# FFN input product of a two-layer encoder: seven half products for eight, over gate/up pairs

## Chip, cores and metric

One core of one Trainium2 chip runs the whole program in one launch. The metric is the device time of that launch in microseconds, lower is better.

## What is computed

A bidirectional encoder of `DEPTH` = 2 layers over T = 528 tokens (16 meta tokens and 512 of the input), model width 1024. Each layer has four token mixers, whose outputs are joined by one output projection, and then the feed-forward part, which is all that the change touches:

```python
def rms_norm(x, g):
    xf = x.astype(jnp.float32)
    y = xf * lax.rsqrt(jnp.mean(xf * xf, axis=-1, keepdims=True) + EPS)
    return (y * g.astype(jnp.float32)).astype(x.dtype)
...
        h = h + mixed @ w_out[l]
        hn = rms_norm(h, ffn_norm_g[l])
        gate, up = jnp.split(hn @ w_ffn_in[l], 2, axis=-1)
        h = h + (jax.nn.silu(gate) * up) @ w_ffn_out[l]
    return h[:, N_META:].astype(x.dtype)
```

`w_ffn_in` is 1024 x 5632: 22 tiles of 128 gate columns and 22 of 128 up columns (`KF` = 22). The last layer needs no meta tokens behind its output projection, so it works on 512 tokens there.

## The kernel before

All is held feature-major: a tile has 128 features on the partitions and the tokens along the free dimension. `h` holds the 8 tiles of the residual stream. Every fp32 product is made as three products of fp32r operands: each operand is split into a lead (the value cast to fp32r) and a rest (value minus lead), and lead x lead, lead x rest and rest x lead are summed in PSUM.

The weights come as a stream of slots of 128 x 1024 (512 KB), one for each output tile of 128 columns. SyncE loads slot by slot into `raw`, which has two places. For each slot ScalarE casts the lead into `parts` (`lead`, L1574), GpSimd subtracts it from the weights to get the rest (`rest`, L651), and TensorE multiplies. `parts` has two places too (`PARTS` = 2), so lead and rest of a slot are made while TensorE works on the slot ahead of it. A lead waits until TensorE has left the place (`w_used`), a load waits until GpSimd has made the rest (`split`).

The order of the work is written out by hand in one block for each engine, and each engine runs its instructions strictly in that order. TensorE's order behind the mixers, for each layer, is:

- eight groups of the second half of the output projection (`G_OUT2`). VectorE adds each to `h` (`residual`, L1944), multiplies by the norm's gain and splits the result into lead and rest (`gains`, L1895 and L1896). ScalarE squares `h` (L1454), VectorE adds the squares up (L1912);
- 44 groups of the FFN input product (`G_FIN`), gate and up in turn. A group is one output tile: 8 input tiles times 3 products. In the first layer the 528 tokens are two matmuls of 264 columns (`product`, L873, two banks of PSUM); in the last layer one of 512 (L908 to L910, one bank). Behind the first group comes the sum for the norm (`residual_sum`), from which ScalarE makes the scale `rstd` (L1474, L1475);
- eight groups of the output product (`G_FOUT`), 22 steps each.

For each gate/up pair j VectorE scales both groups out of PSUM (`scale_out`, L1927, into `ebuf` and `mbuf`), ScalarE applies Silu to the gate (L1862), VectorE multiplies the two (L2473) and splits the product into lead (L2475) and rest (L2476), the operand of the output product.

## Time and profile before

| | |
|---|---|
| median of 3 runs | 2173.76 us (2170.25 to 2173.88) |
| the profiled execution | 2173.68 us, of which 2171.8 us are the span of its instructions |
| TensorE busy | 2023.7 us, 93% of the span |
| GpSimd busy | 1001.7 us, 46% |
| VectorE busy | 1084.3 us, 50% |
| ScalarE busy | 831.0 us, 38% |
| mean granted TensorE clock | 0.986 |
| FFN input product, first layer | 725.9 to 985.9 us of the span |
| FFN input product, last layer | 1798.3 to 2044.1 us of the span |

In the profile an engine's busy time is the time covered by its instructions. PE is TensorE's matmuls, PEld its weight loads, DVE VectorE, ACT ScalarE, POOL GpSimd, SP SyncE. An instruction that has been issued and waits for a resource inside its engine counts as busy, so its row is longer than those of the same form. Times of rows are microseconds from the span's start. L12 is line 12 of the kernel. "pb" is PSUM; every other name is a buffer in SBUF.

### The profile page before, as it was taken

The numbers are of one execution on the slowest core, as the hardware profiler recorded it, in microseconds if no ns is written. First come the engines' busy times: TensorE is split into PE (matmuls) and PEld (weight loads), VectorE is DVE, ScalarE is ACT, GpSimd is POOL, SyncE is SP. The second block draws the span as 40 slices with busy tenths as digits, with TensorE's granted clock in tenths as the row PEclk, the third lists the DMA queues.
The fourth block names the chain that finished last, engine by engine and source line by source line (L and its number), as shares of the span: only waits on it lengthen the run. The fifth ranks groups of instructions, "written<-read, shape, count | busy, mean of one in ns | idle before, by whom it ended". The sixth has DMA issues, their size and how long they took to land.

```text
span 2171.8 us, 32558 instructions
## 1 busy us (share of the span) xinstructions
PE 2023.7 (93%) x13234; PEld 1755.5 (81%) x13234; DVE 1084.3 (50%) x1721; ACT 831.0 (38%) x1364; POOL 1001.7 (46%) x593
## 2 busy tenths in 40 slices
PE   7999998888789999999999999988887899999999
PEld 7988987567668999999999889885665677888887
DVE  7532377666665544441037332676656755444300
ACT  4322343677563222222234222444666622222211
POOL 4365444774323444444434455337853234444443
PEclk9999999999989999999999999999999999999999
DMA  4211111000001222223322111111001022233333
GB/s 168 69 59 59 59 49 69 10 1 30 20 20 59 89 88 93 92 88 97 98 81 85 59 59 59 52 57 40 1 20 30 20 78 97 89 96 97 97 101 113
DMA packets 40325, 143.80 MB, mean 66 GB/s; under 512 B 4592, under 2 KB 4976, under 8 KB 40048
## 3 DMA queue, kind: packets, MB, share of 16 engines
q1 hardware_dynamic: 40176, 141.72, 20.3%
q8 instruction: 106, 1.74, 0.3%
q14 instruction: 43, 0.35, 0.0%
HBM read 139.60 MB, written 2.10 MB: 65 GB/s over the span
## 4 chain that ended last, share of the span: by engine, by line
PE 75%; DVE 12%; ACT 7%; issue 5%; POOL 1%; DMA 0%; SPq 0%; DVEq 0%; ACTq 0%; POOLq 0%
PE pb L873 35%; PE pb L908 7%; PE pb L909 7%; PE pb L910 7%; PE pb L946 4%; PE pb L948 3%; PE pb L947 3%; DVE rowmax L2001 2%; PE pb L1331 1%; PE pb L1323 1%; ACT rstd L1480 1%; ACT ebuf L1515 1%; PE pb L1032 1%; ACT proj_r L1536 1%; POOL parts L651 1%
## 5 line engine op out<-in xcount | busy, mean ns | idle before, releaser
L651 POOL TENSOR_TENSOR parts<-raw,parts 128x1024 fp32r<-128x1024 f32 x248 | 606.8, 2447 | 797.0 <-ACT parts L1574 796.9
L1574 ACT ACTIVATE parts<-raw 128x1024 fp32r<-128x1024 f32 x248 | 262.5, 1058 | 832.3 <-PE pb L873 404.3
L873 PE MATMUL pb<-proj_r,parts 128*128 128x264 f32 x3104 | 427.9, 285 | 0.5 <-POOL parts L651 0.5
L873 PEld LDWEIGHTS pb<-proj_r,parts 128*128 128x128 f32 x3104 | 399.6, 189 | 0.8 <-issue 0.7
L873 PE MATMUL pb<-mix,parts 128*128 128x264 f32 x2208 | 332.5, 292 | 22.6 <-DVE mix L1903 13.6
L873 PEld LDWEIGHTS pb<-mix,parts 128*128 128x128 f32 x2208 | 298.1, 194 | 27.2 <-DVE mix L1903 14.0
L946 PE MATMUL pb<-mix,parts 128*128 128x264 f32 x800 | 242.6, 303 | 1.3 <-DVE proj L1936 1.3
L948 PE MATMUL pb<-mix,parts 128*128 128x264 f32 x800 | 229.5, 287 | 0.0
L947 PE MATMUL pb<-mix,parts 128*128 128x264 f32 x800 | 229.2, 286 | 0.0
L908 PE MATMUL pb<-proj_r,parts 128*128 128x512 f32 x528 | 207.4, 393 | 0.8 <-DVE mbuf L1927 0.8
L910 PE MATMUL pb<-proj_r,parts 128*128 128x512 f32 x528 | 207.7, 393 | 0.0
L909 PE MATMUL pb<-proj_r,parts 128*128 128x512 f32 x496 | 197.3, 398 | 0.0
L946 PEld LDWEIGHTS pb<-mix,parts 128*128 128x128 f32 x800 | 152.9, 191 | 14.2 <-issue 11.8
L1944 DVE TENSOR_TENSOR h<-h,pb 128x528 f32<-128x528 f32 (+1 forms) x48 | 33.1, 691 | 259.0 <-PE pb L910 134.2
L947 PEld LDWEIGHTS pb<-mix,parts 128*128 128x128 f32 x800 | 153.1, 191 | 0.9
L948 PEld LDWEIGHTS pb<-mix,parts 128*128 128x128 f32 x800 | 152.7, 191 | 0.0
L1927 DVE TENSOR_TENSOR mbuf<-pb,rstd 128x528 f32<-128x528 f32 (+1 forms) x44 | 30.8, 699 | 215.1 <-PE pb L873 110.8
L908 PEld LDWEIGHTS pb<-proj_r,parts 128*128 128x128 f32 x528 | 99.2, 188 | 24.9 <-DVE mbuf L1927 1.2
L910 PEld LDWEIGHTS pb<-proj_r,parts 128*128 128x128 f32 x528 | 99.3, 188 | 22.4
L2475 DVE CAST proj_r<-ebuf 128x528 fp32r<-128x528 f32 x44 | 110.8, 2518 | 1.5
L1936 DVE TENSOR_TENSOR proj<-pb,rstd 128x264 f32<-128x264 f32 x100 | 42.6, 427 | 137.9 <-PE pb L948 137.7
L909 PEld LDWEIGHTS pb<-proj_r,parts 128*128 128x128 f32 x496 | 94.0, 189 | 20.8
(290 smaller groups left out, 3291.9 us busy)
## 6 DMA issues: line engine op xcount, KB each, us to landing
raw<-w_stream SPq DMA_DIRECT2D x250, 512.0 KB, 3.5
w_head<-w_heads SPq DMA_DIRECT2D x8, 512.0 KB, 4.0
h<-x_t SPq DMA_DIRECT2D x8, 264.0 KB, 4.6
out_t<-h SPq DMA_DIRECT2D x8, 256.0 KB, 4.9
con<-consts SPq DMA_DIRECT2D x1, 1652.5 KB, 9.7
par<-params SPq DMA_DIRECT2D x1, 170.0 KB, 6.5
par<-params SPq DMA_DIRECT2D x1, 166.0 KB, 5.9
con<-consts SPq DMA_DIRECT2D x1, 128.0 KB, 6.4
```

Source lines behind the costliest of these rows:

```text
L651: nc.gpsimd.tensor_tensor(parts[:, n % PARTS, 1, :], w, parts[:, n % PARTS, 0, :].bitcast(FP32), ALU.subtract).then_inc(split.sem, 1)
L873: last = nc.tensor.matmul(pb[rows_, 2 * p + a, 0:HALF], lhs_t, rhs[:, a * HALF:(a + 1) * HALF], start=start, stop=stop)
L908: nc.tensor.matmul(o, w_lead, lead[:, kept(l, g)], start=(k == 0), stop=False)
L909: nc.tensor.matmul(o, w_lead, rest[:, kept(l, g)], start=False, stop=False)
L910: last = nc.tensor.matmul(o, w_rest, lead[:, kept(l, g)], start=False, stop=(k == k_all - 1))
L946: nc.tensor.matmul(o, w_lead, lead, start=(k == 0), stop=False)
L947: nc.tensor.matmul(o, w_lead, rest, start=False, stop=False)
L948: last = nc.tensor.matmul(o, w_rest, lead, start=False, stop=(k == KD - 1))
L1574: nc.scalar.activation(parts[:, n % PARTS, 0, :], raw[:, r % RAW, :], ACT.Copy).then_inc(lead_ready.sem, 1)
L1936: ins = nc.vector.tensor_tensor(dst[:, cut], pb[:, 2 * bank_pair(g) + a, 0:HALF], rstd[:, cut], ALU.mult)
L2001: link(nc.vector.tensor_reduce(rowmax[:, n % 2:n % 2 + 1], pair(n % 2), AX.XY, ALU.max))
L2475: link(nc.vector.tensor_copy(lead, prod))
```

## The change

The FFN input product is arranged as a 2 x 2 by 2 x 2 block product for each gate/up pair: the weight blocks are gate and up (rows) by the first and second half of the 1024 inputs (A11, A12; A21, A22), the operand blocks are the two halves of the inputs by the first and second half of the tokens. One level of Strassen's scheme (in Winograd's form) makes the four output blocks of 128 x 264 (128 x 256 in the last layer) from seven products in the place of eight. Each of the seven ("half product") is 4 input tiles times 3 matmuls of 264 or 256 columns into one PSUM bank. In the order in which they run their weights are A11, A12, A22, S1, S3, S2, S4 (i = 0 to 6; q = 7j + i), where

S1 = A21 + A22, S3 = A11 - A21, S2 = S1 - A11, S4 = A12 - S2.

- VectorE makes the four weight sums of a pair (`w_sums`, 128 x 512 each), mostly in place in the raw slots.
- Lead and rest are made for half slots (`lead_fin`, `rest_fin`): seven of 128 x 512 on ScalarE and seven on GpSimd for each pair, where there were two of 128 x 1024. `parts` becomes a ring of four half slots (`FIN_RING`).
- The up weights of all pairs use the same place in `raw`; the gate weights alternate between the other place and `sq`. SyncE loads the up weights of a pair when the rest of S3 of the pair before is made.
- The operand has 16 blocks in the place of 8 tiles: first, second, even and odd of each of four pairs of input tiles. ScalarE copies and casts (`x_copy`, `first_lead`, `second_lead`, `summed_lead`), VectorE makes the differences (`first_difference`, `other_differences`) and the rests (`b_rest`). The output projection's second half runs in the order `PAIRED`, so that both tiles of a pair are ready one after the other.
- Out of PSUM, ScalarE copies one product (`fin_copy`) and VectorE makes seven sums of 128 x 264, each of one PSUM bank and one SBUF operand (`fin_sums`), then multiplies gate and up by `rstd` in SBUF (`fin_scaled`). The product's lead is made by ScalarE (`product_lead`) and not by VectorE; the rest stays on VectorE (`product_rest`).
- In ScalarE's order the Silu of pair j - 1 (`gate_silu`) stands behind the lead of S3 and ahead of the lead of S2 of pair j. In VectorE's order the first three weight sums of pair j + 1 stand behind the first sum of pair j.
- Before the first slot of the output product GpSimd clears `kh` and `qh` in the first layer, since they held operand blocks.

The diff, cut to what the prediction speaks of:

```diff
+PAIRED = [f + KD // 2 * b for f in range(KD // 2) for b in range(2)]
+FIN_A11, FIN_A12, FIN_A22, FIN_S1, FIN_S3, FIN_S2, FIN_S4 = range(7)
+N_FIN = 7 * KF
+FIN_RING = 4
+B_FIRST, B_SECOND, B_EVEN, B_ODD = range(4)
...
+        def fin_split_of(layer, q):
+            r = (q + 2 * layer) % FIN_RING
+            return tuple(parts[:, r // 2, b, r % 2 * (SLOT // 2):(r % 2 + 1) * (SLOT // 2)] for b in range(2))
+        def fin_bank(layer, q):
+            return pb[:, (q + 6) % 8, 0:fin_half(layer)]
...
+                j = s - 1 - S_FIN
+                if j == 2:
+                    return added.sem, added.at(l, 2 * KD)
+                if j in (2 * KF, 2 * KF + 1):
+                    return fin_rest.sem, fin_rest.at(l, 7 * (KF - 1) + FIN_S3 + 1 if j % 2 else 7 * (KF - 2) + FIN_S4 + 1)
+                if 2 < j < 2 * KF:
+                    return fin_rest.sem, fin_rest.at(l, 7 * (j // 2 - 1) + FIN_S3 + 1 if j % 2 else 7 * (j // 2 - 2) + FIN_S4 + 1)
...
+                for q in range(N_FIN):
+                    rest_fin(l, q)
+                if l + 1 < DEPTH:
+                    pool.wait_ge(fin_used.sem, fin_used.at(l, N_FIN))
+                    nc.gpsimd.memset(kh[:, :, :], 0.0)
+                    nc.gpsimd.memset(qh[:, :, :], 0.0).then_inc(cleared.sem, 1)
+                for s in range(S_FOUT, N_SLOT):
+                    rest(l, s)
...
+            def fin_product(l, q):
+                j, i = q // 7, q % 7
+                pe.wait_ge(fin_rest.sem, fin_rest.at(l, q + 1))
+                if q in (0, 4, 6):
+                    pe.wait_ge(evac.sem, evac.at(l, G_FIN - {0: 2, 4: 1, 6: 0}[q]))
+                if q == 6:
+                    pe.wait_ge(rs_ready.sem, rs_ready.at(l, RS_F + 1))
+                if j and i == 1:
+                    pe.wait_ge(fin_copied.sem, fin_copied.at(l, j))
+                if j >= 2 and i == 0:
+                    pe.wait_ge(fin_read.sem, fin_read.at(l, 7 * (j - 1)))
+                if j and i in (2, 3, 4):
+                    pe.wait_ge(fin_read.sem, fin_read.at(l, 7 * (j - 1) + {2: 1, 3: 5, 4: 6}[i]))
+                w_lead, w_rest = fin_split_of(l, q)
+                o = fin_bank(l, q)
+                for c in range(KD // 2):
+                    if q < 4:
+                        pe.wait_ge(b_ready_f.sem, b_ready_f.at(l, 4 * c + q + 1))
+                    lead, rest = fin_operand(l, i, c)
+                    nc.tensor.matmul(o, w_lead[:, c * P:(c + 1) * P], lead, start=(c == 0), stop=False)
+                    nc.tensor.matmul(o, w_lead[:, c * P:(c + 1) * P], rest, start=False, stop=False)
+                    last = nc.tensor.matmul(o, w_rest[:, c * P:(c + 1) * P], lead, start=False, stop=(c == KD // 2 - 1))
+                last.then_inc(fin_used.sem, 1)
...
+                for q in range(N_FIN):
+                    fin_product(l, q)
+                    if q == 3:
+                        residual_sum(l, 2)
...
+            def lead_fin(l, q):
+                j, i = q // 7, q % 7
+                if i in (FIN_A11, FIN_A22):
+                    n = l * N_RAW + S_FIN + 1 + 2 * j + (i == FIN_A22)
+                    act.wait_ge(loaded[LOAD_AT[n][0]].sem, LOAD_AT[n][1])
+                if i >= FIN_S1:
+                    act.wait_ge(fin_summed.sem, fin_summed.at(l, 4 * j + i - FIN_S1 + 1))
+                if q < FIN_RING:
+                    act.wait_ge(w_used.sem, w_used.at(l, S_FIN - (1 if q < 2 else 0)))
+                else:
+                    act.wait_ge(fin_used.sem, fin_used.at(l, q - FIN_RING + 1))
+                nc.scalar.activation(fin_split_of(l, q)[0], fin_piece(l, q), ACT.Copy).then_inc(fin_lead.sem, 1)
...
+            def fin_copy(l, j):
+                act.wait_ge(fin_used.sem, fin_used.at(l, 7 * j + FIN_A11 + 1))
+                if j:
+                    act.wait_ge(fin_read.sem, fin_read.at(l, 7 * (j - 1) + 4))
+                nc.scalar.activation(fin_first[:, 0:fin_half(l)], fin_bank(l, 7 * j + FIN_A11), ACT.Copy).then_inc(fin_copied.sem, 1)
+            def gate_silu(l, j):
+                act.wait_ge(evac.sem, evac.at(l, G_FIN + 2 * j + 1))
+                g = ebuf[:, j % 2, 0:2 * fin_half(l)]
+                nc.scalar.activation(g, g, ACT.Silu).then_inc(gsilu.sem, 1)
+            def product_lead(l, j):
+                act.wait_ge(act_product.sem, act_product.at(l, j + 1))
+                nc.scalar.activation(act_parts(j)[0][:, fin_cut(l)], ebuf[:, j % 2, 0:2 * fin_half(l)], ACT.Copy).then_inc(act_lead.sem, 1)
...
                 for k in range(KD):
-                    lead(l, S_OUT2 + k + 2)
+                    if k < KD - 2:
+                        lead(l, S_OUT2 + k + 2)
+                    elif k == KD - 2:
+                        lead_fin(l, 0)
+                        lead_fin(l, 1)
+                    else:
+                        lead_fin(l, 2)
                     act.wait_ge(evac.sem, evac.at(l, G_OUT2 + k + 1))
+                    if k % 2 == 0:
+                        x_copy(l, k // 2)
+                        first_lead(l, k // 2)
+                    else:
+                        second_lead(l, k // 2)
+                        summed_lead(l, k // 2, B_EVEN)
+                        summed_lead(l, k // 2, B_ODD)
+                    if k == KD - 1:
+                        lead_fin(l, 3)
                     residual_square(l, 1, k)
-                residual_rstd(l, 1)
-                nc.scalar.preload_act_table_set("silu_and_others")
-                for j in range(KF):
-                    lead(l, S_FIN + 2 * j + 2)
-                    act.wait_ge(evac.sem, evac.at(l, G_FIN + 2 * j + 1))
-                    nc.scalar.activation(ebuf[:, j % 2, :], ebuf[:, j % 2, :], ACT.Silu).then_inc(gsilu.sem, 1)
-                    lead(l, S_FIN + 2 * j + 3)
+                for q in range(FIN_RING, N_FIN):
+                    j, i = q // 7, q % 7
+                    lead_fin(l, q)
+                    if i == 4:
+                        fin_copy(l, j)
+                        if j == 0:
+                            residual_rstd(l, 1)
+                            nc.scalar.preload_act_table_set("silu_and_others")
+                        else:
+                            gate_silu(l, j - 1)
+                    if i == 6 and j:
+                        product_lead(l, j - 1)
+                lead(l, S_FOUT)
+                lead(l, S_FOUT + 1)
+                gate_silu(l, KF - 1)
+                product_lead(l, KF - 1)
...
+            def w_sums(l, j, n):
+                gate, up, w = fin_gate(l, j), fin_up(l, j), SLOT // 2
+                a11, a12, a21, a22, s1 = gate[:, 0:w], gate[:, w:], up[:, 0:w], up[:, w:], fin_sum(j)
+                if n == 0:
+                    r = l * N_RAW + S_FIN + 1 + 2 * j
+                    dve.wait_ge(loaded[LOAD_AT[r + 1][0]].sem, LOAD_AT[r + 1][1])
+                    dve.wait_ge(loaded[LOAD_AT[r][0]].sem, LOAD_AT[r][1])
...
+                    if j > 1:
+                        dve.wait_ge(fin_rest.sem, fin_rest.at(l, 7 * (j - 1) + FIN_S1 + 1))
+                    ins = nc.vector.tensor_tensor(s1, a21, a22, ALU.add)
+                elif n == 1:
+                    ins = nc.vector.tensor_tensor(a21, a11, a21, ALU.subtract)
+                elif n == 2:
+                    dve.wait_ge(fin_rest.sem, fin_rest.at(l, 7 * j + FIN_A11 + 1))
+                    dve.wait_ge(fin_summed.sem, fin_summed.at(l, 4 * j + 2))
+                    ins = nc.vector.tensor_tensor(a11, s1, a11, ALU.subtract)
+                else:
+                    dve.wait_ge(fin_rest.sem, fin_rest.at(l, 7 * j + FIN_A12 + 1))
+                    dve.wait_ge(fin_summed.sem, fin_summed.at(l, 4 * j + 3))
+                    ins = nc.vector.tensor_tensor(a12, a12, a11, ALU.subtract)
+                ins.then_inc(fin_summed.sem, 1)
+            def fin_sums(l, j, n):
+                w = fin_half(l)
+                first, g, up = fin_first[:, 0:w], ebuf[:, j % 2, 0:2 * w], mbuf[:, j % 2, 0:2 * w]
+                i, own, dst, after = ((FIN_A12, first, g[:, 0:w], None), (FIN_S2, first, first, 1), (FIN_S3, first, up[:, w:2 * w], 2),
+                                      (FIN_S1, first, g[:, w:2 * w], 2), (FIN_A22, up[:, w:2 * w], up[:, 0:w], 3),
+                                      (FIN_S1, up[:, w:2 * w], up[:, w:2 * w], 5), (FIN_S4, g[:, w:2 * w], g[:, w:2 * w], 4))[n]
+                dve.wait_ge(fin_used.sem, fin_used.at(l, 7 * j + (i if n in (0, 6) else FIN_S2) + 1))
+                if n == 0:
+                    dve.wait_ge(fin_copied.sem, fin_copied.at(l, j + 1))
+                else:
+                    dve.wait_ge(fin_read.sem, fin_read.at(l, 7 * j + after))
+                nc.vector.tensor_tensor(dst, fin_bank(l, 7 * j + i), own, ALU.add).then_inc(fin_read.sem, 1)
+            def fin_scaled(l, j, buf):
+                at = buf[:, j % 2, 0:2 * fin_half(l)]
+                dve.wait_ge(fin_read.sem, fin_read.at(l, 7 * j + 7))
+                nc.vector.tensor_tensor(at, at, rstd[:, fin_cut(l)], ALU.mult).then_inc(evac.sem, 1)
...
+                    if k == KD - 1:
+                        for n in range(4):
+                            w_sums(l, 0, n)
+                    residual(l, G_OUT2 + k, PAIRED[k])
+                    if k % 2 == 0:
+                        first_difference(l, k // 2)
+                        b_rest(l, k // 2, B_FIRST)
+                    else:
+                        other_differences(l, k // 2)
+                        b_rest(l, k // 2, B_SECOND)
+                        b_rest(l, k // 2, B_EVEN)
+                        b_rest(l, k // 2, B_ODD)
                     add_square(l, 1, k)
                 dve.wait_ge(rs_ready.sem, rs_ready.at(l, RS_F + 1))
                 for j in range(KF):
-                    if j >= 2:
-                        dve.wait_ge(act_ready.sem, act_ready.at(l, j - 1))
-                    scale_out(l, G_FIN + 2 * j, ebuf[:, j % 2, :])
-                    scale_out(l, G_FIN + 2 * j + 1, mbuf[:, j % 2, 0:T])
+                    fin_sums(l, j, 0)
+                    if j + 1 < KF:
+                        for n in range(3):
+                            w_sums(l, j + 1, n)
+                    if j:
+                        product_rest(l, j - 1)
+                    for n in range(1, 6):
+                        fin_sums(l, j, n)
+                    if j + 1 < KF:
+                        w_sums(l, j + 1, 3)
+                    fin_sums(l, j, 6)
+                    fin_scaled(l, j, ebuf)
+                    fin_scaled(l, j, mbuf)
                     dve.wait_ge(gsilu.sem, gsilu.at(l, j + 1))
                     dve.wait_ge(evac.sem, evac.at(l, G_FIN + 2 * j + 2))
-                    prod = ebuf[:, j % 2, :]
-                    link(nc.vector.tensor_tensor(prod, prod, mbuf[:, j % 2, 0:T], ALU.mult))
-                    lead, rest = act_parts(j)
-                    link(nc.vector.tensor_copy(lead, prod))
-                    nc.vector.tensor_tensor(rest, prod, lead.bitcast(FP32), ALU.subtract).then_inc(act_ready.sem, 1)
+                    prod = ebuf[:, j % 2, 0:2 * fin_half(l)]
+                    nc.vector.tensor_tensor(prod, prod, mbuf[:, j % 2, 0:2 * fin_half(l)], ALU.mult).then_inc(act_product.sem, 1)
+                product_rest(l, KF - 1)
```

## Rows read from the trace of the kernel before

**Rows 1.** The page: busy time and instructions by engine.

```profile
PE 2023.7 (93%) x13234; PEld 1755.5 (81%) x13234; DVE 1084.3 (50%) x1721; ACT 831.0 (38%) x1364; POOL 1001.7 (46%) x593
```

**Rows 2.** Busy time by stretch: both input products, and attention.

```profile
core 0: us, PE busy (x) PEld busy (x) DVE busy (x) ACT busy (x) POOL busy (x), PEclk, DMA share, GB/s
725.90:985.90 260.00, 259.47 (x2118) 259.16 (x2117) 117.74 (x110) 61.61 (x70) 109.08 (x44) 1.00 0.28 90
1798.30:2044.10 245.80, 244.96 (x1058) 198.36 (x1057) 117.14 (x110) 61.58 (x70) 109.23 (x44) 1.00 0.30 94
...
1497.00:1650.00 153.00, 125.34 (x604) 92.00 (x604) 91.53 (x185) 99.94 (x195) 95.53 (x70) 1.00 0.03 11
```

**Rows 3.** Timeline (start, length) of VectorE: one pair of each layer.

```profile
809.94 0.71 DVE L1927 TENSOR_TENSOR mbuf<-pb,rstd 128x528 f32<-128x528 f32 x1 [5.09 <-PE pb L873]
...
821.69 0.71 DVE L1927 TENSOR_TENSOR mbuf<-pb,rstd 128x528 f32<-128x528 f32 x1 [5.10 <-PE pb L873]
...
1900.77 0.69 DVE L1927 TENSOR_TENSOR mbuf<-pb,rstd 128x512 f32<-128x512 f32 x1 [4.80 <-PE pb L910]
...
1911.89 0.69 DVE L1927 TENSOR_TENSOR mbuf<-pb,rstd 128x512 f32<-128x512 f32 x1 [4.80 <-PE pb L910]
```

**Rows 4.** Timeline of TensorE: 264 columns into one bank.

```profile
186.12 0.29 PE L947 MATMUL pb<-mix,parts 128*128 128x264 f32 x1
...
188.33 0.28 PE L947 MATMUL pb<-mix,parts 128*128 128x264 f32 x1
```

**Rows 5.** Timeline of GpSimd and VectorE, both with two SBUF operands.

```profile
292.09 2.37 POOL L651 TENSOR_TENSOR parts<-raw,parts 128x1024 fp32r<-128x1024 f32 x1 [3.61 <-ACT parts L1574]
...
292.53 2.48 DVE L2254 TENSOR_TENSOR proj<-proj,con 128x528 f32<-128x528 f32 x1
...
294.41 1.78 POOL L801 TENSOR_TENSOR proj<-proj,con 128x528 f32<-128x528 f32 x1
...
306.71 1.18 POOL L794 TENSOR_TENSOR o_tok<-o_tok,kh 128x512 f32<-128x512 f32 x1 [1.82 <-ACT kh L1658]
...
307.26 1.20 DVE L2233 TENSOR_TENSOR sq<-sq 128x528 f32<-128x528 f32 x1 [1.33 <-ACT sq L1448]
...
307.84 1.77 POOL L801 TENSOR_TENSOR proj<-proj,con 128x528 f32<-128x528 f32 x1
```

**Rows 6.** The same view, VectorE with an operand in PSUM.

```profile
261.28 2.38 POOL L651 TENSOR_TENSOR parts<-raw,parts 128x1024 fp32r<-128x1024 f32 x1 [6.78 <-ACT parts L1574]
...
261.82 0.69 DVE L2218 TENSOR_TENSOR kh<-pb,con 128x516 f32<-128x516 f32 x1 [1.30 <-PE pb L1184]
```

**Rows 7.** Groups by line and shape: busy us, mean ns.

```profile
L651 POOL TENSOR_TENSOR parts<-raw,parts 128x1024 fp32r<-128x1024 f32 x248 | 606.8, 2447 | 797.0 <-ACT parts L1574 796.9
...
L681 POOL TENSOR_TENSOR proj_r<-proj,mix 128x512 fp32r<-128x512 f32 x3 | 3.8, 1276 | 0.2
...
L1936 DVE TENSOR_TENSOR proj<-pb,rstd 128x264 f32<-128x264 f32 x100 | 42.6, 427 | 137.9 <-PE pb L948 137.7
...
L2476 DVE TENSOR_TENSOR mix<-ebuf,proj_r 128x528 fp32r<-128x528 f32 x32 | 22.7, 709 | 1.1
...
L1496 ACT ACTIVATE mbuf<-o_tok 128x512 f32<-128x512 f32 x10 | 6.2, 616 | 0.0
...
L644 POOL MEMSET mbuf<- 128x1280 f32 x1 | 1.2, 1168 | 0.0
```

**Rows 8.** The page: a weight load, KB, median us to landing.

```profile
raw<-w_stream SPq DMA_DIRECT2D x250, 512.0 KB, 3.5
```

**Rows 9.** Timeline of ScalarE behind the norm's sum.

```profile
734.25 1.28 ACT L1858 ACT_TABLE_LOAD   x1
```

**Rows 10.** Timeline of TensorE behind a stretch without work.

```profile
1739.80 0.77 PE L908 MATMUL pb<-mix,parts 128*128 128x512 f32 x1 [2.91 <-POOL parts L651]
...
1740.37 0.63 PE L909 MATMUL pb<-proj_r,parts 128*128 128x512 f32 x1
...
1740.79 0.63 PE L910 MATMUL pb<-mix,parts 128*128 128x512 f32 x1
```

217 lines of the change are left out of this document (160 added, 57 removed).

## Prediction

> **What bounds the kernel now.** The page comes first: TensorE is busy 93% of the span, no other engine over half of it [rows 1]. Busy time by stretch then shows that in both FFN input products it is 259.5 of 260.0 us and 245.0 of 245.8 us, at a granted clock of 1.00, the 2.4 GHz level [rows 2]. VectorE's timeline gives the beat of a gate/up pair: 821.69 - 809.94 = 11.75 us in the first layer, 1911.89 - 1900.77 = 11.12 us in the last [rows 3]. A pair is 96 matmuls of 264 columns (122.4 ns each) or 48 of 512 (231.7 ns). So TensorE sets the beat; VectorE and GpSimd have 117 and 109 us of work in each stretch, 45% [rows 2]. Less work on TensorE is a gain only as long as nobody else sets a longer beat.
>
> **TensorE's part.** A half product is 12 matmuls into one bank. Into one bank, 18 matmuls of 264 columns take 188.33 - 186.12 = 2.21 us, 122.8 ns each [rows 4], so the bank order costs nothing. First layer: 84 x 122.4 = 10.28 us a pair, 1.47 less than before. Last layer: 84 of 256 columns. That form is in no row; it lies between 122.4 x 256/264 = 118.7 ns and 122.4 ns, and I take 118.9, on the line through the 264 and 512 column prices: 9.99 us a pair, 1.13 less. Were TensorE still the bound, 22 x (1.47 + 1.13) = 57 us would go.
>
> **What the others get.** GpSimd: seven rests of 128x512 at 1.276 us and 0.07 between them [rows 7], 9.4 us a pair for 4.9. ScalarE: seven leads and a Silu at 0.62, a copy at about 0.4, the product's lead at 0.7, by the 0.616 for 512 columns [rows 7], 6.3 us with its gaps. VectorE: seven sums of 264 columns with an operand in PSUM at 0.427 (I call them U) and eight instructions with both operands in SBUF (L): four weight sums, two scalings, the product, its rest, at 0.71 for 528 columns; idle before each is 1.1/32 = 0.03 [rows 7]. That is 7 x 0.47 + 8 x 0.74 = 9.2 us. Each alone fits under 10.28 us. Together they don't, for one reason.
>
> **The port.** A VectorE instruction with two SBUF operands doesn't run beside a two-operand GpSimd instruction. The one at 292.53 takes 2.48 us where its kind takes 0.71; it ends at 295.01, 0.55 after GpSimd's ended at 294.46. GpSimd's next, begun at 294.41, ends at 296.19; GpSimd's ends are 1.73 us apart, and 1.72 at 307.84, where 1.31 (1.276 for 528 columns) + 0.07 = 1.38 would do [rows 5, 7]. So an L caught behind a running rest ends 0.55 after it, and puts 0.34 on GpSimd; one following another alternate with the rests at 1.61 to 1.67 us each. With an operand in PSUM there is no such wait: 0.69 us in the midst of a 2.38 us rest [rows 6]. Before, this hit the cast and some rests and was hidden.
>
> The Trainium skill (SBUF — State Buffer, "SBUF: two separate sides") says the same and more: the pair of ports is an exclusive lock for the whole instruction. By that alone a pair would need 7 x 1.276 + 8 x 0.70 = 14.5 us of port. The rows show that 0.3 to 0.4 us of each L hides in the turn-over, so the sum goes by the rows.
>
> By the rows the port needs at least 7 x 1.35 + 7 x 0.34 + 0.74 = 12.6 us a pair (seven gaps for eight L; without the slower alternations seen, 12.4). Over both old beats already.
>
> **The order on each engine makes it longer.** I lay out one pair of the first layer from the diff's order, with these prices; each number is the time in us at which the step ends, counted from the moment VectorE has scaled the gate of pair j-1. ScalarE stood there waiting for that (the Silu of j-1), with the leads of S2 and S4 of pair j queued behind it: Silu 0.73, the two leads 1.4 and 2.0, product lead 2.7, then the leads of j+1 at 3.4, 4.0 and on, each early enough. VectorE and GpSimd, in the order in which they hold the port: up scaling 0.75, product 1.5, U 2.0. Rest S2: 1.5 to 2.65 (held by the product). Weight sum 0 of j+1 waits for it: 3.2. Rest S4 4.3; weight sum 1 4.85. Rest A11 of j+1 5.95. Weight sum 2 needs that rest done, but GpSimd's next is ready 0.07 later and gets in first: A12 7.3, weight sum 2 7.85. Rest A22 8.95, product rest 9.5. Rest S1 10.6, beside it five U 11.85 (queued behind every L above). Rest S3 11.95, weight sum 3 12.5. U 12.95, gate scaled 13.7. So VectorE's chain, with GpSimd between its links, gives **13.7 us**; 13.0 if weight sum 2 gets in first. TensorE's waits fit (S1 and S3 of the next pair need the fifth and sixth sum of this one, 11.4 and 11.85, and end at 14.4), and the up weights, asked for at 11.95 of the pair before, land 3.5 later [rows 8], at 1.8, ahead of weight sum 0. In the last layer columns are 3% fewer on U and half the L: 13.4 us. TensorE then idles a quarter of the time, in gaps of up to 2 us.
>
> **Ends of the stretch.** At the start the operand blocks of the last input tiles follow the last residual: residual and ScalarE's lead 1.6, three differences of 264 columns (about 0.5 each) behind a rest 3.4, the rest of the second block 4.1, then cast and rest of the even block 4.9 and of the odd block 5.6, lead and rest of S1 7.0: the fourth half product ends 8.5 after the output projection, where 4 x 1.47 = 5.9 would do. The norm's sum 9.1, its scale 10.5 and the table load (1.28) [rows 9] 11.8 stand in ScalarE ahead of S2's lead; S2's product ends at 15.3, and with the five U, weight sum 3 and the last U behind it the first gate is scaled at about 19.5 us. In the output projection VectorE's work for two groups is about 6.2 of L and 1.5 of U, and it stands behind two rests of 2.45 [rows 7] for up to 4.4: 12.1 for the 11.7 us that TensorE needs. I put 1 us a layer, between nothing and 3. At the end the last half product ends 6.0 after the last but one gate is scaled; then, first layer only, GpSimd waits for it, clears 1056 and 1280 columns (1.168 for 1280 [rows 7]: 2.1) and makes the first rest of the output product (2.45): 4.7 us of TensorE idle; last layer 0.9. The tail of sums, Silu and split of the last pair hides behind the 21 steps ahead of it in the output product (15 us). Behind 2.91 us of idleness TensorE ran matmuls of 512 columns 0.42 us apart, the 1.2 GHz level, not 0.23 [rows 10]; I put 3 us for that behind the 4.7. The steady gaps are shorter, and in attention, TensorE busy 125 of 153 us, the clock stayed at 1.00 [rows 2], so I charge nothing there.
>
> **The sum**, against the profiled 2173.68 us (the median is 2173.76). First layer: 19.5 + 20 x 13.7 + 6.0 + 4.7 = 304.2 for 260.0, +44. Last: 19.5 + 20 x 13.4 + 5.9 + 0.9 = 294.3 for 245.8, +48.5. With 2 + 3: +98. **2271 us**, slower by 4.5%.
>
> **Rivals.**
> 1. *The port is packed without loss* and GpSimd's rests follow each other always: 12.5 us and 12.3. 40 periods less 1.15: 2271 - 46 = 2225. For it: the layout has GpSimd free from 11.95 to 13.7 only since ScalarE waits in the Silu. Against it: that wait is in the order. 15%.
> 2. *GpSimd wins twice*: where a link waits for VectorE's own result or a lead comes early, a second rest gets in ahead of an L. One more such loss a pair is 1.35 us, 40 of them 54, with some in the output projection: 2325 to 2335. 14%.
> 3. *No port cost for these shapes*: the same layout without waits still has Silu, two leads, three rests (5.4) ahead of weight sum 2, then 0.75 x 2, 2.35, 0.75, 0.47, 0.75: 11.2 us, for 11.75 and 11.12. With 18 us to the first gate: 18 + 20 x 11.2 + 10.7 = 252.7 and 18 + 20 x 11.1 + 6.8 = 246.8, and 5: 1 us less than 505.8, or 2172, the same. 5%.
> 4. *TensorE stays the bound*: 10.28 and 9.99 us. With 8 us for the start in each layer and the ends of the forecast, 8 + 22 x 10.28 + 4.7 and 8 + 22 x 9.99 + 0.9: 238.9 + 228.7 + 5 = 472.6 for 505.8, 2140 us, faster. It decides if the sum of L and rests with their turn-over is under 10 us; the rows say 12.4. A place where I could be wrong is the weight sums in raw and sq. 8%.
>
> **How the numbers follow.** My case 58%, then 15, 14, 5, 8. The range for 8 in 10 takes in the packed port and most of the double loss: 2215 to 2335. Faster by over 0.2% (about what a measurement of this kernel can tell from no change) has the 8 of rival 4, within it the 5 of rival 3, slower the rest: 0.08, 0.05, 0.87.
>
> **What would show it.** After the change the weight sums, scalings and product rests (two SBUF operands) should average 1.1 to 1.6 us and not 0.7, the PSUM sums stay at 0.43. Rests of 128x512 should be 1.3 alone and up to 1.7 held. The beat should be 13 to 14.4 us in both layers alike, TensorE at about 75% in the stretch, waiting for GpSimd's rests and for VectorE's sums, ScalarE's longest waits at the Silu. If the L stay at 0.7 beside running rests, rival 4 or 3 holds; if GpSimd has no gap at all, rival 1. A beat of 10.3 would prove me wrong.

## The result and the profile after

The changed kernel takes 2281.39 us in the median (2278.64 to 2283.97) where the kernel before takes 2173.82: a ratio of 1.0496, 95% interval 1.0481 to 1.0511. The forecast was 2271 us within 2215 to 2335. The profiled execution took 2283.97 us, its span 2282.0 us, 110.2 more than the span before (2171.8).

The page of the changed kernel, beside [rows 1]:

```profile
PE 2030.9 (89%) x13762; PEld 1780.5 (78%) x13762; DVE 1362.7 (60%) x2193; ACT 980.8 (43%) x1712; POOL 1251.5 (55%) x815
```

TensorE is busy as long as before in all, over a longer span. Busy time by stretch, from the first half product to the first matmul of the output product in each layer, beside [rows 2]:

```profile
core 0: us, PE busy (x) PEld busy (x) DVE busy (x) ACT busy (x) POOL busy (x), PEclk, DMA share, GB/s
730.30:1038.80 308.50, 252.57 (x1854) 237.69 (x1853) 261.85 (x337) 129.42 (x228) 234.53 (x156) 0.97 0.25 76
1854.10:2156.50 302.40, 252.52 (x1853) 238.66 (x1852) 253.48 (x333) 124.89 (x224) 230.67 (x153) 0.94 0.25 77
```

VectorE's busy time went from 118 to 262 us and GpSimd's from 109 to 235: their own work, 9.2 and 9.4 us a pair by the forecast's prices, is 202 and 207 us. Where the rest comes from shows in one pair of the first layer, VectorE first, then GpSimd (start, length; "x2" is two instructions shown together; L2175, L2169 and L2171 are weight sums, L2206 is the rest of the product, L2194 a sum out of PSUM, L2200 the scaling, L2800 the product; L775 is a rest):

```profile
856.57 1.77 DVE L2175 TENSOR_TENSOR sq<-rstd,sq 128x512 f32<-128x512 f32 x1 [1.19 <-POOL parts L775]
858.26 1.80 DVE L2206 TENSOR_TENSOR mix<-ebuf,proj_r 128x528 fp32r<-128x528 f32 x1
859.98 0.42 DVE L2194 TENSOR_TENSOR fin_first<-pb,fin_first 128x264 f32<-128x264 f32 x1
...
863.38 0.71 DVE L2200 TENSOR_TENSOR ebuf<-ebuf,rstd 128x528 f32<-128x528 f32 x1
...
865.16 0.71 DVE L2800 TENSOR_TENSOR ebuf<-ebuf,mbuf 128x528 f32<-128x528 f32 x1 [0.46 <-ACT ebuf L1773]
...
866.13 1.42 DVE L2169 TENSOR_TENSOR rstd<-raw 128x512 f32<-128x512 f32 x1
867.47 1.78 DVE L2171 TENSOR_TENSOR raw<-raw 128x512 f32<-128x512 f32 x1
870.44 1.76 DVE L2175 TENSOR_TENSOR raw<-rstd,raw 128x512 f32<-128x512 f32 x1 [1.19 <-POOL parts L775]
```

```profile
857.73 1.75 POOL L775 TENSOR_TENSOR parts<-raw,parts 128x512 fp32r<-128x512 f32 x1
859.44 1.77 POOL L775 TENSOR_TENSOR parts<-rstd,parts 128x512 fp32r<-128x512 f32 x1
861.18 1.28 POOL L775 TENSOR_TENSOR parts<-raw,parts 128x512 fp32r<-128x512 f32 x1
865.37 3.34 POOL L775 TENSOR_TENSOR parts<-sq,parts 128x512 fp32r<-128x512 f32 x2 [2.91 <-ACT parts L1740]
```

An instruction with two SBUF operands takes 1.4 to 1.8 us where a rest runs, and 0.71 in the 2.91 us in which GpSimd waits for ScalarE; a rest takes 1.28 us alone and 1.75 beside one of them. I call such a stretch, in which the two engines hold each other up, a turn on the port. The sums that read PSUM stay at 0.42. The waits in 770 to 1030 us (total, times, longest) show who stands behind whom:

```profile
POOL parts L775 <- ACT parts L1740: 58.2, 20, 2.9
PEld pb L1101 <- POOL parts L775: 57.4, 71, 2.3
...
ACT ebuf L1773 <- DVE ebuf L2200: 47.2, 20, 2.4
PE pb L1101 <- POOL parts L775: 35.5, 20, 2.1
```

Once a pair ScalarE waits 2.4 us at the Silu for the scaled gate (L1773), GpSimd then 2.9 for the lead behind it, and TensorE for GpSimd's rests (L1101).

### The profile page after: what moved, and what is told of

It is laid out like the page before. It is cut to its first block, busy times and chain, and to the rows that moved or that the text cites. A ratio compares the mean times of both kernels' runs of the same rounds, so it can differ in the third digit from the quotient of the medians.

```text
span 2282.0 us, 35406 instructions
## 1 busy us (share of the span) xinstructions
PE 2030.9 (89%) x13762; PEld 1780.5 (78%) x13762; DVE 1362.7 (60%) x2193; ACT 980.8 (43%) x1712; POOL 1251.5 (55%) x815
## 4 chain that ended last, share of the span: by engine, by line
PE 51%; DVE 20%; POOL 10%; issue 9%; ACT 7%; DMA 2%; SPq 0%; DVEq 0%; ACTq 0%; POOLq 0%
PE pb L1004 22%; POOL parts L775 8%; PE pb L1074 4%; PE pb L1076 3%; PE pb L1075 3%; PE pb L1037 3%; PE pb L1038 3%; PE pb L1039 3%; DMA raw<-w_stream 2%; DVE mix L2206 2%; DVE rowmax L2310 2%; PE pb L1484 1%; PE pb L1476 1%; ACT rstd L1630 1%; DVE ebuf L2200 1%
## 5 line engine op out<-in xcount | busy, mean ns | idle before, releaser
L769 POOL TENSOR_TENSOR parts<-raw,parts 128x1024 fp32r<-128x1024 f32 x160 | 390.5, 2441 | 500.2 <-ACT parts L1726 500.0
L1004 PE MATMUL pb<-mix,parts 128*128 128x264 f32 x2208 | 336.1, 294 | 21.9 <-DVE mix L2212 12.9
L1726 ACT ACTIVATE parts<-raw 128x1024 fp32r<-128x1024 f32 x160 | 169.0, 1056 | 427.7 <-PE pb L1004 195.9
L1101 PE MATMUL pb<-proj_r,parts 128*128 128x264 f32 (+1 forms) x792 | 246.1, 311 | 94.9 <-POOL parts L775 78.7
L1004 PEld LDWEIGHTS pb<-mix,parts 128*128 128x128 f32 x2208 | 301.8, 196 | 26.5 <-DVE mix L2212 13.3
L775 POOL TENSOR_TENSOR parts<-raw,parts 128x512 fp32r<-128x512 f32 x176 | 264.0, 1514 | 81.2 <-ACT parts L1740 80.9
L1101 PEld LDWEIGHTS pb<-proj_r,parts 128*128 128x128 f32 x792 | 155.3, 196 | 122.8 <-POOL parts L775 121.8
L1103 PE MATMUL pb<-proj_r,parts 128*128 128x264 f32 (+1 forms) x792 | 229.7, 290 | 0.0
L1102 PE MATMUL pb<-proj_r,parts 128*128 128x264 f32 (+1 forms) x704 | 204.0, 290 | 0.0
L2253 DVE TENSOR_TENSOR h<-h,pb 128x528 f32<-128x528 f32 (+1 forms) x48 | 33.1, 689 | 256.2 <-PE pb L1039 129.3
L1004 PE MATMUL pb<-proj_r,parts 128*128 128x264 f32 x1024 | 172.1, 288 | 5.0 <-POOL parts L769 5.0
L775 POOL TENSOR_TENSOR parts<-sq,parts 128x512 fp32r<-128x512 f32 x88 | 129.8, 1495 | 61.6 <-ACT parts L1740 61.6
L1103 PEld LDWEIGHTS pb<-proj_r,parts 128*128 128x128 f32 x792 | 155.4, 196 | 0.0
L1004 PEld LDWEIGHTS pb<-proj_r,parts 128*128 128x128 f32 x1024 | 145.6, 192 | 5.2 <-issue 5.2
L1740 ACT ACTIVATE parts<-raw 128x512 fp32r<-128x512 f32 x176 | 105.8, 623 | 101.5 <-PE pb L1103 74.5
L1102 PEld LDWEIGHTS pb<-proj_r,parts 128*128 128x128 f32 x704 | 138.2, 196 | 0.1
```

The source lines that it names most:

```text
L769: nc.gpsimd.tensor_tensor(parts[:, b, 1, :], w, parts[:, b, 0, :].bitcast(FP32), ALU.subtract).then_inc(split.sem, 1)
L775: nc.gpsimd.tensor_tensor(other, fin_piece(l, q), lead.bitcast(FP32), ALU.subtract).then_inc(fin_rest.sem, 1)
L1004: last = nc.tensor.matmul(pb[rows_, 2 * p + a, 0:HALF], lhs_t, rhs[:, a * HALF:(a + 1) * HALF], start=start, stop=stop)
L1101: nc.tensor.matmul(o, w_lead[:, c * P:(c + 1) * P], lead, start=(c == 0), stop=False)
L1102: nc.tensor.matmul(o, w_lead[:, c * P:(c + 1) * P], rest, start=False, stop=False)
L1103: last = nc.tensor.matmul(o, w_rest[:, c * P:(c + 1) * P], lead, start=False, stop=(c == KD // 2 - 1))
```

## The experiments

All start from the changed kernel and were measured beside the kernel before. "Beat" is the mean distance of two Silus over the first 20 pairs, first and last layer; "opening" is from the first half product to the first Silu; "between" is from the fourth matmul before the end of the first layer's input product to the first half product of the last layer. These come from the profiled execution, and so does the time ahead of the first half product. That time lay between 724.9 and 730.3 us in the 13 kernels, whose instructions are the same up to the output projection: so much a profiled span differs by itself, and the stretches tell more than the spans. Of e2 and e4 there is one run each.

| kernel | median us | ratio to before (95%) | beat | opening | between |
|---|---|---|---|---|---|
| changed kernel | 2281.4 | 1.0496 (1.0481 to 1.0511) | 13.53, 13.44 | 25.7, 26.7 | 821.1 |
| e0_seven_banks | 2280.8 | 1.0485 (1.0469 to 1.0501) | 13.51, 13.43 | 25.7, 26.4 | 822.4 |
| e1_port_all | 2157.3 | 0.9916 (0.9899 to 0.9932) | 10.42, 10.47 | 25.6, 26.6 | 823.3 |
| e2_port_weights | 2196.3 | one run | 11.38, 11.22 | 25.6, 26.5 | 823.7 |
| e3_sum3_late | 2272.1 | 1.0444 (1.0422 to 1.0466) | 13.31, 13.23 | 25.5, 26.5 | 820.3 |
| e4_silu_late | 2277.9 | one run | 13.41, 13.31 | 26.2, 27.2 | 823.0 |
| e5_clear_late | 2274.1 | 1.0457 (1.0431 to 1.0484) | 13.51, 13.52 | 25.5, 25.1 | 814.8 |
| o1_opening | 2276.6 | 1.0468 (1.0441 to 1.0494) | 13.52, 13.48 | 21.7, 21.8 | 822.9 |
| f1_copies | 2186.1 | 1.0055 (1.0037 to 1.0073) | 11.29, 11.29 | 23.6, 24.7 | 821.7 |
| f2_three | 2177.0 | 1.0007 (0.9998 to 1.0016) | 11.20, 11.22 | 21.2, 21.2 | 815.0 |
| g1_silu_mid | 2224.5 | 1.0220 (1.0206 to 1.0234) | 12.37, 12.30 | 21.2, 21.1 | 820.6 |
| g2_silu_late | 2226.5 | 1.0225 (1.0211 to 1.0239) | 12.38, 12.30 | 21.2, 21.1 | 820.0 |
| h1_scale_in_psum | 2163.4 | 0.9949 (0.9935 to 0.9963) | 10.93, 11.00 | 21.5, 21.6 | 816.6 |

### Is it the port? (e0, e1, e2)

The waits on the port can't be taken away by themselves, but what makes them can: the second operand is read from PSUM. The eight banks are all in the ring, so the ring is first cut to seven (e0), with TensorE's waits moved to match, which leaves bank 5 idle.

> The changed kernel with the half products going round seven PSUM banks in place of eight, nothing else (a control for the next two). TensorE's wait for a bank comes one product earlier: the wait for the fifth PSUM sum now stands ahead of product 2 of the next pair. That sum ends about 1.5 us before TensorE gets there in the profile of the changed kernel, so both theories expect next to nothing: a beat of the gate scalings of 13.5 to 13.7 us in the first layer and 2276 to 2290 us.

```diff
-            return pb[:, (q + 6) % 8, 0:fin_half(layer)]
+            return pb[:, (0, 1, 6, 7, 2, 3, 4)[q % 7], 0:fin_half(layer)]
```

2280.8 us and the same beat: the control is neutral. Then as many instructions of the same sizes, with one operand from the idle bank. They take the smaller of the two values, so the results are not the network's:

```diff
+            def two_sbuf(j, out, a, b, op):
+                other = idle_bank(j, a.shape[-1])
+                if other is None:
+                    return nc.vector.tensor_tensor(out, a, b, op)
+                return nc.vector.tensor_tensor(halves(out), halves(a), other, ALU.min)
...
-                    ins = nc.vector.tensor_tensor(s1, a21, a22, ALU.add)
+                    ins = two_sbuf(j, s1, a21, a22, ALU.add)
```

> The seven banks of the control, and all eight VectorE instructions of a pair that read two SBUF operands (four weight sums, two scalings, the product, its rest) read one operand from the idle PSUM bank instead, and take the smaller of the two in place of the sum, difference or product, for pairs 2 to 18 of 20 in each layer. Those values are therefore not the network's. Same count of instructions, same sizes, same waits. The port theory: VectorE and GpSimd no longer take turns, VectorE has 7 x 0.43 + 8 x 0.71 = 8.7 us and GpSimd 7 x 1.28 = 8.9 us a pair, and what is left is the chain of the layout without its port waits: a beat of 11.2 us in the first layer and 11.0 in the last, so 34 x 2.4 = 80 us less than the control, about 2200 us (2185 to 2220); rests of 1.28 us each, weight sums of 0.7. The rival (the length of the order of handovers, with the port having little part): the beat stays above 13 us and the time above 2265 us.

> As the kernel with all eight, but only the four weight sums of a pair read the idle PSUM bank (and take the smaller value, so that the weights of the S products of pairs 2 to 18 are wrong); the two scalings, the product and its rest keep two SBUF operands. By the port theory each two-SBUF instruction that meets a rest costs 0.55 to 1.1 us, and the weight sums meet the rests more often than the scalings do: a beat of 11.6 us (11.3 to 12.2), about 2215 us (2200 to 2240). By the rival: above 13 us and above 2265 us.

The two texts miscount: there are 22 pairs a layer, and 19 of each (2 to 20) read the bank, 38 in all. e1 took 123.5 us less than its control, 3.25 for each of the 38, and 19 us less than the kernel before beside it (2176.4); e2 84.6 us less, 2.2 for each. Both times stand far under the rival's 2265 us: the port theory holds and the rival is out. The operation was changed along with the operand's place, but not its length: 681 ns, where a weight sum of the changed kernel that meets no rest takes 0.68 us (L2169 at 729.37). The weight sums alone give two thirds of what the eight give. The size was forecast too small, though: 80 us were expected. Groups of e1, 780 to 990 us (busy us, mean ns):

```profile
L2165 DVE TENSOR_TENSOR ebuf<-ebuf,pb 128x528 f32<-128x528 f32 x36 | 25.3, 704 | 2.8 <-ACT ebuf L1771 0.5
L2165 DVE TENSOR_TENSOR raw<-raw,pb 128x512 f32<-128x512 f32 x33 | 22.5, 681 | 2.5 <-POOL parts L775 2.5
...
L775 POOL TENSOR_TENSOR parts<-raw,parts 128x512 fp32r<-128x512 f32 x70 | 90.2, 1307 | 12.4 <-ACT parts L1738 12.4
```

and its busy time, with that of the changed kernel below it:

```profile
780.00:980.00 200.00, 193.16 (x1570) 192.59 (x1569) 147.92 (x276) 103.72 (x182) 165.15 (x129) 0.99 0.32 98
```

```profile
780.00:980.00 200.00, 165.44 (x1229) 154.41 (x1229) 175.10 (x222) 82.19 (x149) 156.36 (x105) 0.99 0.26 80
```

VectorE 74%, GpSimd 83% and TensorE 97% busy at once. The distance of two Silus is 10.19 us in the first layer and 10.09 in the last in the median; the means of the table also hold the first and last pairs, which don't read the bank. That is TensorE's own time: from 780 to 940 us of the first layer it has no gap. So 3.25 us a pair is what could be won before TensorE set the beat, and not all that the port costs.

The Trainium skill (SBUF — State Buffer, "SBUF: two separate sides") names the condition: VectorE takes the shared pair with two SBUF inputs, against a GpSimd instruction that reads SBUF. The run agrees: 681 ns beside running rests with one SBUF operand, up to 1.8 us with two.

### The order of the links (e3, e4)

```diff
-                        for n in range(3):
+                        for n in range(2):
                             w_sums(l, j + 1, n)
                     if j:
                         product_rest(l, j - 1)
+                    if j + 1 < KF:
+                        w_sums(l, j + 1, 2)
```

> Every value as in the changed kernel; VectorE's order alone is changed: weight sum 2 (which waits for GpSimd's rest of the first half slot and is followed by the rest of the product) is put behind the rest of the product. The port theory: VectorE no longer waits some 1 us for GpSimd there, and the rest of the product takes the port in that time: a beat of 12.85 us (12.4 to 13.5), 26 us less, about 2255 us (2240 to 2281). By the rival that the chain through the weight sums and the S products sets the beat, with weight sum 2 on it: the beat grows by the 0.7 to 1.8 us of the rest of the product, 14.2 to 15 us, 2310 us or more.

The beat is 12.89 us in one pair of three and 13.50 in most others: 9 us gained of 26. VectorE's wait for GpSimd is gone in both kinds, and the rival's longer beat didn't come. In the slower kind another wait stands in its place:

```profile
864.29 1.76 DVE L2169 TENSOR_TENSOR rstd<-raw 128x512 f32<-128x512 f32 x1 [0.83 <-DMA raw<-w_stream]
865.97 1.79 DVE L2171 TENSOR_TENSOR raw<-raw 128x512 f32<-128x512 f32 x1
867.68 1.79 DVE L2206 TENSOR_TENSOR mix<-ebuf,proj_r 128x528 fp32r<-128x528 f32 x1
869.40 1.77 DVE L2175 TENSOR_TENSOR raw<-rstd,raw 128x512 f32<-128x512 f32 x1
...
877.09 1.22 DVE L2169 TENSOR_TENSOR rstd<-raw 128x512 f32<-128x512 f32 x1
```

The first four rows are of a slower pair, the last of a faster one. In the 13 slower pairs from 757 to 1011 us VectorE waits 0.8 to 1.9 us for the up weights' load ahead of weight sum 0 (L2169); in the 7 faster ones 0.17 us at most. The three instructions behind it stand 1.8 us each beside a rest in both kinds. By these rows it is the landing of the up weights that kept most pairs of e3 from the shorter beat. They are asked for behind the rest of S3 of the pair before; no run asks for them earlier, so this is not shown.

e4 moves the other wait of the beat, ScalarE's at the Silu:

```diff
-                        else:
-                            gate_silu(l, j - 1)
                     if i == 6 and j:
+                        gate_silu(l, j - 1)
                         product_lead(l, j - 1)
```

> Every value right; ScalarE takes the Silu of the pair before just ahead of the lead of its product, behind the leads of S2 and S4, instead of ahead of these two. In the profile ScalarE waits 2.4 us a pair at the Silu for VectorE's scaling of the gate, with the two leads queued behind it. The port theory: VectorE and GpSimd set the beat by the turns they take; the leads come sooner, but VectorE's chain is as long: a beat of 13.2 to 13.6 us, 2270 to 2284 us. The rival, that ScalarE's wait at the Silu sets the beat by making GpSimd's rests late: a beat of 12.5 us or less, about 2240 us.

0.12 us a pair, in one run. Both orders leave the number of turns on the port as it is, and the beat nearly so: the packed port of my first rival, 12.5 us, was not reached by either.

### The two ends (e5, o1)

```diff
-                if l + 1 < DEPTH:
-                    pool.wait_ge(fin_used.sem, fin_used.at(l, N_FIN))
-                    nc.gpsimd.memset(kh[:, :, :], 0.0)
-                    nc.gpsimd.memset(qh[:, :, :], 0.0).then_inc(cleared.sem, 1)
                 for s in range(S_FOUT, N_SLOT):
                     rest(l, s)
+                    if l + 1 < DEPTH and s == S_FOUT + 1:
+                        pool.wait_ge(fin_used.sem, fin_used.at(l, N_FIN))
...
```

> Every value right; GpSimd's two clears of kh and qh (0.98 and 1.17 us), which stand between the last half product and the first rest of the output product in the first layer, are put behind the rests of the first two slots. TensorE's idle time there falls from 4.99 to 2.9 us. If the slow stretch behind it (some 4.7 us at the 1.2 GHz level) stays as it is, 2.1 us less, 2279 us; if the shorter gap lets the clock stay, 4.5 us less, 2277 us. The rival, that the clears were hidden: no change.

The time between the input products falls from 821.1 to 814.8 us, by more than either number. GpSimd and TensorE in the changed kernel:

```profile
1033.89 0.98 POOL L993 MEMSET kh<- 128x1056 f32 x1 [3.12 <-PE pb L1103]
1034.81 1.17 POOL L994 MEMSET qh<- 128x1280 f32 x1
1035.93 5.53 POOL L769 TENSOR_TENSOR parts<-raw,parts 128x1024 fp32r<-128x1024 f32 x2
```

```profile
1038.82 0.78 PE L1004 MATMUL pb<-proj_r,parts 128*128 128x264 f32 x2 [4.99 <-POOL parts L769]
1039.39 0.64 PE L1004 MATMUL pb<-mix,parts 128*128 128x264 f32 x2
```

and with the late clears, where the last half product's matmul starts at 1030.60:

```profile
1027.93 2.36 POOL L769 TENSOR_TENSOR parts<-raw,parts 128x1024 fp32r<-128x1024 f32 x1
```

```profile
1030.60 0.42 PE L1103 MATMUL pb<-o_tok_r,parts 128*128 128x264 f32 x1
1030.82 0.44 PE L1004 MATMUL pb<-proj_r,parts 128*128 128x264 f32 x2
```

For e5 I had counted the clears, not the wait ahead of them. That wait, 3.12 us for the last half product, stood ahead of the first rest too, which doesn't need it; with it moved, the rest is made beside the half products, and the whole idle time of 4.99 us is gone. With it goes the slow stretch behind it: in the changed kernel the first 22 matmuls after the gap are 0.22 us apart (the 1.2 GHz level) and the others 0.12, and the granted clock is 0.87 in the 27 us from 1033, where e5 has 0.98 in the 27 us from 1030.

```diff
                     if k == KD - 1:
-                        for n in range(4):
+                        for n in range(2):
                             w_sums(l, 0, n)
...
+                for n in (2, 3):
+                    w_sums(l, 0, n)
...
-                        if j == 0:
-                            residual_rstd(l, 1)
-                            nc.scalar.preload_act_table_set("silu_and_others")
+                    if q == 6:
+                        residual_rstd(l, 1)
+                        nc.scalar.preload_act_table_set("silu_and_others")
```

> Every value right; only the opening of the FFN input product is put in another order. VectorE makes weight sums 2 and 3 of the first pair (the second of them took 1.59 us beside a rest) after the last residual's work instead of ahead of it, and ScalarE takes the leads of the sixth and seventh half product ahead of the norm's two passes and the table load instead of behind them. I had the first gate scaled 19.5 us after the output projection ends; it was 25.7. My theory: the missing 6.2 us are the 2.3 that the two weight sums hold the last residual up and about 3.5 that the two leads wait behind the norm and the table load. So the first gate is scaled at 19.5 to 21 us in both layers, 10 to 12 us less in all: 2270 us (2265 to 2275). The rival: the opening is bound by the norm's sum and scale themselves, which the half products with all seven banks wait for: under 4 us less, 2277 us or more.

The opening falls by 4.0 and 4.9 us, between the two theories. The median falls by 4.8 us, between them too, and by less than the two openings together. So the orders I named cost about two thirds of the missing 6.2 and 7.1 us. These are the places in the changed kernel, VectorE, ScalarE and TensorE:

```profile
731.55 1.59 DVE L2179 TENSOR_TENSOR raw<-raw 128x512 f32<-128x512 f32 x1
733.06 0.69 DVE L2253 TENSOR_TENSOR h<-h,pb 128x528 f32<-128x528 f32 x1
```

```profile
743.22 1.28 ACT L2084 ACT_TABLE_LOAD   x1
744.51 1.15 ACT L1740 ACTIVATE parts<-raw 128x512 fp32r<-128x512 f32 x2
```

```profile
735.82 0.39 PE L1101 MATMUL pb<-o_tok_r,parts 128*128 128x264 f32 x1 [2.77 <-DVE o_tok_r L2127]
747.10 0.59 PE L1101 MATMUL pb<-proj_r,parts 128*128 128x264 f32 x1 [3.85 <-POOL parts L775]
```

The last residual (L2253) stands behind two more weight sums, the leads (L1740) behind the table load; in o1 the two gaps of TensorE are 1.36 and 0.21 us, with 0.42 between them, and another of 1.17 follows. Something else goes with the gaps. These are the openings of the changed kernel and, below them, of o1:

```profile
730.30:756.00 25.70, 19.09 (x128) 18.54 (x127) 15.93 (x24) 11.40 (x19) 14.30 (x10) 0.87 0.20 62
1854.10:1880.80 26.70, 20.16 (x127) 19.58 (x126) 16.15 (x25) 11.35 (x20) 14.23 (x10) 0.81 0.19 60
```

```profile
724.90:746.60 21.70, 18.54 (x142) 17.57 (x141) 17.12 (x24) 11.44 (x20) 14.46 (x10) 1.00 0.23 74
1845.20:1867.00 21.80, 18.27 (x141) 17.16 (x140) 17.07 (x25) 11.38 (x20) 14.56 (x10) 1.00 0.23 73
```

The granted clock was 0.87 and 0.81 in the openings of the changed kernel, and 1.00 in both of o1: behind the gap of 3.21 us in the last layer the matmuls are 0.21 us apart and not 0.12. So part of the 4.0 and 4.9 us may be the clock, which neither theory named; no run parts it from the order. What holds the opening at 21.7 us was not tried.

### A correct kernel with fewer turns (f1, f2, g1, g2, h1)

e1 says what to build: have ScalarE put one operand of each weight sum into the idle bank. Banks are given over whole, since the Trainium skill (PSUM — Partial Sum Buffer, "PSUM bank collisions raise a hardware error") says that two engines may not access one bank within the same partition at the same time; no run here tries it.

```diff
+            def w_copy(l, j, n):
+                gate, up, w = fin_gate(l, j), fin_up(l, j), SLOT // 2
+                src = (up[:, 0:w], gate[:, 0:w], gate[:, w:])[n]
...
+                nc.scalar.activation(pb[:, 5, 0:w], src, ACT.Copy).then_inc(w_copied.sem, 1)
...
                     lead_fin(l, q)
+                    if j and i < 3:
+                        w_copy(l, j, i)
```

> Every value right. The seven banks of the control, and ScalarE copies three weight quarters of a pair into the idle eighth bank, one after the other (the lower half of the up slot after the lead of the first half slot, the gate's after the second, its other half after the third), so that all four weight sums of pairs 1 to 21 read one operand from PSUM; the rest of the product of the pair before is put ahead of weight sum 0. The port theory, by the run with the weight sums alone on the idle bank (11.13 us a pair): a beat of 11.1 to 11.5 us, since ScalarE has 6 us of work a pair and 1.9 more fit in; 40 beats times 2.2 less than the control, 2192 us (2180 to 2215). The rival: the three copies, each between two steps of the chain load, weight sum, weight sum, put about 0.7 us each into a chain that TensorE waits for: 12.5 us or more, above 2235 us.

As forecast: 11.13 us in most pairs, 95.3 us less than the changed kernel. The copies (0.60 us each) cost nothing that the beat shows: in e2, which frees the same turns without them, it is 11.12 us in most pairs. The three together (f1, e5 and o1):

> Every value right; the copies into the idle bank, the late clears and the new order of the opening together. By the stretches of the three runs: the copies gave 47.8 and 45.9 us in the two FFN input products, 2.1 of each in the opening; the late clears 6.3 us behind the first; the new opening 4.0 and 4.9, of which I count half, since the copies had shortened the opening already. From the 2186.1 us of the copies: less 6.3 and less 4.5 is 2175 us (2169 to 2181), level with the kernel before. If the parts give all that they gave alone: 2171. Beat as with the copies alone, 11.1 us.

2177.0 us, level with the kernel before (0.9998 to 1.0016). Then the Silu, which looked like the next wait:

```diff
-                        if j:
-                            gate_silu(l, j - 1)
+                    if i == 5 and j:
+                        gate_silu(l, j - 1)
```

> Every value right; as the three together, and ScalarE takes the Silu of the pair before behind the lead of S2 and ahead of that of S4, in place of ahead of both. In the profile of the copies ScalarE stands 2.6 us a pair in that Silu's wait and GpSimd then 1.84 us for the lead of S2, and TensorE 0.4 to 1.1 us twice a pair for GpSimd's rests. With most of the port's turns gone, my theory is that this wait is now what is left over TensorE's 10.18 us: a beat of 10.4 to 10.7 us, 40 x 0.6 = 24 us less than the three together, 2151 us (2142 to 2162). The rival, that the two scalings, the product and its rest on the port hold the 11.13 us whatever ScalarE does, as in the changed kernel, where a later Silu gave 0.13 us a pair: 5 us less, 2168 us or more.

> Every value right; as the last one, but the Silu stands behind the lead of S4 too, right ahead of the lead of the product. Both rests that followed the Silu can now start early; in exchange ScalarE has nothing between the Silu and the product's lead and waits some 0.7 us there for VectorE's product, with the leads of the next pair queued behind it. My theory has GpSimd's rests S2 and S4 as the late ones: a beat of 10.3 to 10.7 us, 2150 us (2140 to 2165), within 6 us of the kernel with the Silu between them. The rival, as for that one: 2168 us or more.

Both theories fell: 47.5 and 49.5 us slower than f2, a beat of 12.4. VectorE, GpSimd and the waits of ScalarE (780 to 980 us) in g1:

```profile
869.34 1.31 DVE L2219 TENSOR_TENSOR ebuf<-ebuf,rstd 128x528 f32<-128x528 f32 x1
870.57 1.80 DVE L2219 TENSOR_TENSOR mbuf<-mbuf,rstd 128x528 f32<-128x528 f32 x1
872.47 1.61 DVE L2821 TENSOR_TENSOR ebuf<-ebuf,mbuf 128x528 f32<-128x528 f32 x1
```

```profile
870.03 3.48 POOL L776 TENSOR_TENSOR parts<-sq,parts 128x512 fp32r<-128x512 f32 x2
```

```profile
ACT proj_r L1789 <- DVE ebuf L2821: 36.3, 16, 2.3
ACT ebuf L1784 <- DVE ebuf L2219: 30.4, 16, 1.9
```

and the same place in f2:

```profile
870.55 0.69 DVE L2219 TENSOR_TENSOR mbuf<-mbuf,rstd 128x528 f32<-128x528 f32 x1
871.35 0.71 DVE L2821 TENSOR_TENSOR ebuf<-ebuf,mbuf 128x528 f32<-128x528 f32 x1
871.91 1.30 POOL L776 TENSOR_TENSOR parts<-raw,parts 128x512 fp32r<-128x512 f32 x1 [1.84 <-ACT parts L1739]
```

With the leads early the rests run beside the two scalings and the product, which take 4.7 us in place of about 3.0. ScalarE, in order, now waits 2.3 us for the product ahead of its lead, with the next pair's leads behind it. In f2 the Silu's wait kept GpSimd idle for 1.84 us just while VectorE held the port: a wait of one engine was the cover of another's work. That is read from these rows; no run tests it by itself, and the same move in the changed kernel (e4) cost nothing. (Both also lost 5 us again between the input products; in g1 TensorE is idle 2.83 us ahead of the first layer's output product, where f2 has 0.71. That was not followed up.) So the turns themselves have to go; the last kernel takes the scalings' off:

```diff
+                    ins = nc.scalar.activation(pb[:, 0, 0:512], rstd[:, a:a + 512], ACT.Copy)
...
-                nc.vector.tensor_tensor(at, at, rstd[:, fin_cut(l)], ALU.mult).then_inc(evac.sem, 1)
+                ins = nc.vector.tensor_tensor(at[:, 0:512], at[:, 0:512], pb[:, 0, 0:512], ALU.mult)
+                if fin_half(l) > 256:
+                    ins = nc.vector.tensor_tensor(at[:, 512:], at[:, 512:], rstd[:, 512:T], ALU.mult)
+                ins.then_inc(evac.sem, 1)
```

> Every value right; as the three together (Silu where the changed kernel has it), and the two scalings of a pair read the norm's scale from a PSUM bank too, where ScalarE copies its first 512 columns once a layer; the 16 columns over in the first layer are scaled from SBUF by a small instruction of their own. The half products go round six banks, the norm's sum takes the two idle ones first. Left on the port in a pair: seven rests, the product and its rest (and 32 columns). The port theory: 7 x 1.28 + 2 x 0.71 = 10.4 us of port in place of 11.8, with TensorE's 10.18 us just under it: a beat of 10.4 to 10.7 us in the first layer and 10.3 to 10.6 in the last, 41 x 0.6 = 25 us less than the three together, 2152 us (2145 to 2165), 1.1% under the kernel before. The rival, by the two runs with the Silu moved, that ScalarE's wait at the Silu now decides and freeing the scalings only moves the collisions to other rests: 11.0 us or more, above 2170 us; and if six banks are too few, TensorE's waits for VectorE's sums show it.

2163.4 us, ratio 0.9949 (0.9935 to 0.9963): half a per cent faster than the kernel before. The time is inside the range expected. The beat of 10.9 and 11.0 us is above its range and at the rival's 11.0, though the rival's time (above 2170) didn't come. The gate's scaling stands at 687 ns. The excess over 10.19 us shows mostly in two rows of waits, for GpSimd (TensorE's weight loads) and for VectorE's sums. The second is 0.6 us in f2: six banks let TensorE run into those sums.

```profile
PEld pb L1103 <- POOL parts L776: 10.5, 18, 1.0
...
PE pb L1103 <- DVE mbuf L2225: 7.2, 18, 0.8
```

From the first half product to the output product it takes 247.7 and 249.2 us, where the stretches before took 260.0 and 245.8 [rows 2]: the gain is all in the first layer. In the last, Strassen saves TensorE 1.0 us a pair (11.12 to 10.09 in e1) and the opening and the beat take it back.

## Why the prediction was right, step by step

| step | forecast | measured |
|---|---|---|
| seven half products on TensorE alone | 10.28, 9.99 us | 10.19, 10.09 (e1) |
| PSUM sum, 264 columns | 0.427 | 0.42 to 0.43 |
| two SBUF operands, mean of a pair | 1.1 to 1.6 | 1.20 |
| a rest, alone and held | 1.3, 1.7 | 1.28, 1.75 |
| beat | 13.7, 13.4 | 13.53, 13.44 |
| fourth half product ends after the output projection | 8.5 | 10.6, 12.0 |
| product S2 ends | 15.3 | 19.8, 19.7 |
| first gate scaled after the output projection | 19.5 | 25.7, 26.6 |
| last but one gate to the last half product's end | 6.0 | 7.3, 7.0 |
| idle ahead of the output product, first layer | 4.7 | 4.99 |
| slower clock behind it | 3 | 2.9 (815.3 us from there to the last layer's first half product, for 812.4), of which the slow matmuls themselves are 2.2 |
| TensorE's share of the stretch | about 75% | 82, 84% busy in the rows |
| output projection, a layer | +1 | -0.1 in the first layer, +0.2 in the last |
| sum | +98 | +110.2 (profiled spans) |

*The port and the order* were right in mechanism and size. The laid-out pair named what waits for what: the Silu's wait of ScalarE, weight sum 2 behind two rests (1.19 us idle, then 1.76), the product's rest held (1.80), the product at its bare 0.71. Its steps came where it had them: counted from the scaled gate, in the median of 19 pairs weight sum 1 ends at 4.81 us (forecast 4.85), weight sum 2 at 7.76 (7.85), the product's rest at 9.48 (9.5), weight sum 3 at 12.42 (12.5), the next gate at 13.51 (13.7). e1 and e2 show that the port is the cause, and not only beside it.

TensorE's busy share in the rows is above my 75% since a matmul's row is longer than the distance to the next one (0.28 for 0.12 us); by the beat it works 10.19 of 13.53 us, 75%. My sign for ScalarE was half right: it waits 47.2 us at the Silu in 20 pairs, but 50.1 us in 45 short waits for TensorE to leave the ring. My 13.0, "if weight sum 2 gets in first", did not occur; e3, which puts the product's rest ahead of weight sum 2 and so takes VectorE's wait away, gave 12.9 in a third of the pairs.

*The opening* is the term that was mis-sized, by 6.2 and 7.1 us. The step that failed is "the fourth half product ends 8.5 after the output projection ... S2's product ends at 15.3". All four weight sums stand ahead of the last residual, which I read in the diff and did not charge: the fourth half product ended at 10.6 and 12.0 us. The leads behind the norm and table load cost TensorE 3.85 us of idle time: product S2 ended 4.5 and 4.4 us late. I charged nothing for the clock, which was 0.87 and 0.81 there. And from S2's product to the scaled gate I had 4.2 us, where it took 5.9 and 6.9. o1 gives 4.0 and 4.9 us back. In it S2's product ends at 12.6 and 12.5 us, ahead of the forecast, and the gate is still scaled at 21.7: that last part stays open.

*The rest of the 12 us*: first layer 6.2 (opening) - 3.5 (beats) + 1.6 (end) = 4.3 of 308.5; last 7.1 + 0.7 + 0.3 = 8.1 of 302.4. The output projection cost nothing (46.69 us for 46.76 in the first layer, 44.6 for 44.5 in the last), so its 2 go. 4.4 us lie ahead of it, in work that is the same in both kernels, and 2.2 were gained behind the last FFN input product; such differences are in the spread of the profiled spans, and no run explains them.

*The rivals.* The packed port (12.5 us) was out of reach even for e3 and e4. The doubly lost turn didn't happen. Rival 3 is the one whose number was wrong: I laid out 11.2 us for the same order without a port, and e1 measured 10.19, TensorE's own time, in its place. The chain without port waits is shorter than TensorE's, so no port cost would have meant rival 4: its 2140 us agree with e1, 2157.3 less 3.25 for each of the 6 pairs left out, 2138. That error is why the expectation of e1 missed by 43 us, and it had no part in the forecast. By the same 3.25 us for all 44 pairs the port was worth 143 us (an estimate), more than the whole loss.

## What to carry to other kernels

Before work is moved from TensorE to VectorE and GpSimd, count the two-SBUF-operand instructions of both together and not each engine's busy share: here 9.2 and 9.4 us a pair, each under TensorE's 10.3, made 13.5. Such a turn is bought off by an operand in PSUM, even if ScalarE has to copy it there (0.60 us for a turn of up to 1.8), while another order of the same turns gives little or takes much. An idle engine in front of a wait may be what keeps a shared resource free, so a wait is moved only after asking what will then run beside what; and a wait that guards one instruction holds all behind it (the clears: 2.1 us of work, 6.3 of time).

## What the hardware showed that I had not expected

- Three engines at 74, 83 and 97% busy, TensorE with hardly a wait, once VectorE reads PSUM: 681 ns for 512 columns amid rests of 1307 ns.
- Sixteen columns with two SBUF operands still take VectorE 0.17 us in h1 (L2233), where 512 take 0.68: a remainder that is split off is not free. One of the gate's took 1.8 us.
- In the last layer of the changed kernel the granted clock was 0.94 over the stretch and TensorE idle 50 of 302 us, in gaps of 2 us; in attention, TensorE idle 28 of 153 us, it had been 1.00 [rows 2]. I had charged nothing for it. As TensorE was not the bound the beat shows nothing of it (13.44 us); the openings may hold some of it, as o1 shows.
